# Summing four value pages of sample attention in four column strips of the matrix array

## The chip, the cores and the metric

One Trainium2 chip, one of its cores. The metric is the device time of one execution in microseconds (us), lower is better. Before the change three executions took 3119.28, 3115.47 and 3117.53 us: median 3117.53.

## The reference, cut to what matters

One step of a hybrid decoder layer: 2048 prompt tokens and 8 sample tokens go through the same weights (input projection, an RG-LRU group and a differential-attention group, output projection, gated FFN, gated per-layer embeddings). The change lies in the attention of the 8 sample tokens against their paged cache. Each has 4 pages of 128 past tokens, 4 heads, and 128 values per head:

```python
v_past = cache_v[i][page_table].reshape(db, n_pages * PAGE_SIZE, ATT_HEADS, 2 * ATT_HD)
...
w = probs(q1, k1) - lam * probs(q2, k2)
return jnp.einsum('bhqk,bkhe->bqhe', w, v.astype(jnp.float32))
...
o = _rmsnorm(o, lw['subln_g'], eps=1e-5) * (1.0 - lam_init)
```

So for each sample token (a "row" below) and each head, the output is a weighted sum of 512 cached value vectors and of the token's own, then normed over its 128 elements.

## The kernel before, in words

The kernel has three stages: `project` (input projection, LRU), `attend_first` (attention of the first 512 prompt tokens) and `feed` (output projection, FFN and embeddings of all four groups of 512 tokens, with the attention of groups 1 to 3 and of the samples woven in). The change is in `feed`, which runs from about 679 us to the end.

`feed` writes the order of the work out by hand. `ALL` is a list of 345 items: for each group i the items `mix0`, `mix1`, `mix1t`, `near`, `far`, `gate`/`up` of each FFN block b, `down` of each part, `proj`, `pg`. Each engine's program loops over n, the index in `ALL`, and issues its share of item n. On TensorE an ordinary item is 24 products into the four banks `c_bank` (L2613), each item needing one new weight chunk of 128x1024 elements, of which TensorE takes high and low halves: ScalarE rounds a chunk to its high half (L2041), VectorE subtracts to get the low half (L2292), SyncE loads it two items ahead (L1860).

Into this list two other pieces of work are hung by item number:

- Sample attention. `MULT_S` places the score products, `SOFT` = 18 the softmax, and `VAL_S` = 21, 22, 24, 25, 27, 28, 30, 31 the value products of sample rows 0 to 7, each ahead of that item's own products. `FINISH` = 31. For each row there are four f32 matmuls, one for each page: stationary `wz[:, b, j]` (128 keys x 32, only row b's four columns non-zero), moving `pages` (128 keys x 512 = 4 heads x 128 values), all accumulated in `OT[0:32]`, one half of the PSUM tensor `b_S` (L2885). The profile shows two MATMUL instructions for each of these f32 matmuls, 64 in all. Partition r of the result is row r // 4, head r % 4; all four heads' values stand in it and only a quarter is wanted.
- At item `FINISH` VectorE multiplies `OT[0:32]` by a 0/1 tile `head` and sums over the four head positions (L2577, L2579), adds the token's own value (L2581), squares and sums (L2583, L2584). At `FINISH + 1` ScalarE takes the root (L2258), VectorE inverts and scales (L2587, L2588). At `FINISH + 2` TensorE transposes (L2889) and VectorE scales into `res` (L2591). At `FINISH + 3` SyncE stores `res` (L1990).
- SyncE loads the value pages into three buffers: those of row b + 3 are issued at item `VAL_S[b]` + 1 once row b's matmuls are done (L1895).
- Prompt attention of groups 1 to 3. Its 144 steps (group g, head h, tile t, key block kc) are hung as "ticks" on `PLACES`, the `gate`, `up`, `down` and first `pg` items of groups 0 to 2:

```python
PLACES = [n for n in PLACES if n > FINISH + 3]
tick_at = {PLACES[k * len(PLACES) // NTICK]: k for k in range(NTICK)}
```

With 171 places and 150 ticks, 21 places stay without a tick. Tick k computes the scores of step k at the head of its item (L2905, L2907), the maximum (L2499) and the exponential (L2219); half way through the item the weights of an earlier step (2, 3 or 4 ticks before for g = 1, 2, 3) are transposed (L2917, which waits for VectorE's L2492), split by ScalarE and VectorE (L2233, L2517) and at the end of the item multiplied with the values (L2931, L2933, which wait for L2517). One and two ticks after a tile's last value product its output is gathered; at every fourth tile (a "head end") ScalarE takes a root (L2246, with a table load), VectorE scales all four tiles (L2539) and TensorE transposes them at the start of the next tick (L2866). There are 12 head ends. In `gate` items VectorE and ScalarE also carry the SwiGLU of the `up` item before (L2404, L2406, L2238, L2521, L2119).

At the head of `feed` VectorE clears some tiles and makes `pair` and `head` out of the identity (L2279 to L2286).

Of the kernel before, what the change touches and what calls it, by code (L numbers as in the profile page):

```python
# [10 lines left out]
ALU = mybir.AluOpType  # L11
ACT = mybir.ActivationFunctionType
AX = mybir.AxisListType.X

P = 128
# [5 lines left out]
NS = 8  # L21
# [5 lines left out]
HEADS = 4  # L27
# [5 lines left out]
PAGES = 4  # L33
# [1354 lines left out]
def feed(nc, io, split, sems, pool_turn, shared, early, cached, first_stored):  # L1388
# [4 lines left out]
    ident, ident_r, mask, nlam, sub_gain = shared  # L1393
    w, raw, mixA, raw_in, split_hi, split_ready = early
    pages, qb, table, table_in, pages_in, qb_in, free = cached
# [89 lines left out]
    PLACES = [n for n, (i, item) in enumerate(ALL) if i < LAST and (item[0] in ("gate", "up", "down") or item[:2] == ("pg", 0))]  # L1485
    R, RH, W = NS * COMP, NS * HEADS, HEADS * P
# [1 line left out]
    SOFT = MULT_S[-1] + 1  # L1488
    VAL_S = [SOFT + 3 + 3 * b // 2 for b in range(NS)]
    FINISH = VAL_S[-1]  # L1490
    PLACES = [n for n in PLACES if n > FINISH + 3]
    tick_at = {PLACES[k * len(PLACES) // NTICK]: k for k in range(NTICK)}
    assert len(tick_at) == NTICK
    step_of_value = {s + LAG(s): s for s in range(NSTEP)}
# [74 lines left out]
    with ctx:  # L1569
        top = [nc.sbuf_base + -nc.sbuf_base % 64]  # L1570

        def sb(name, shape, dt=F32, offset=None):
            size = int(np.prod(shape[1:])) * (2 if dt == mybir.dt.bfloat16 else 4)
            if offset is None:
                offset, top[0] = top[0], top[0] + size + -size % 32
            return nc.alloc_sbuf_tensor_at(name, shape, dt, offset=offset)
# [27 lines left out]
        p = sb("b_p", [P, PRING, 2, 512])  # L1604
        wT = sb("b_wT", [P, 2, 512], F32R)
        o = sb("b_o", [P, TILES, P])
# [22 lines left out]
        v32 = sb("d_v32", [RH, P])  # L1629
# [3 lines left out]
        cp = sb("d_cp", [P, PAGES * R])  # L1633
        wz = sb("d_wz", [P, NS, PAGES, RH])
        pair = sb("d_pair", [R, RH])
        head = sb("d_head", [RH, HEADS])
        wo = sb("d_wo", [RH, 1])
        mine = sb("d_mine", [RH, HEADS, P])
        os_ = sb("d_o", [RH, P])
        osq = sb("d_osq", [RH, P])  # L1640
        d_ss = sb("d_ss", [RH, 1])
# [202 lines left out]
        def _(sp):  # L1844
# [74 lines left out]
            for n, (i, item) in enumerate(ALL):  # L1919
                if item == ("mix0", 1):  # L1920
                    wait_if_any(sp, x2_ready, TILES * i)
                    for t in range(2):
                        load_row(x_v, i, t)
                    if i == LAST:

                        sp.wait_ge(stored, 16 * NH)
                        sp.dma_start(s_xr[:], x_s).then_inc(s_in, 16)
                        sp.dma_start(s_pin[:], p_s).then_inc(s_in, 16)
                if item == ("mix1", 0) and i:
                    sp.wait_ge(y_ready, TILES * i)  # L1930
                    load_gain(1)
                if item == ("mix1t", 3):
                    sp.wait_ge(x1_ready, nth(i, 0))
                    load_row(x_v, i, 2)
                if item == ("near", 0):
                    sp.wait_ge(x1_ready, nth(i, 1))
                    load_row(x_v, i, 3)
                if item == ("gate", 2):
                    sp.wait_ge(hn_ready, TILES * i + len(tiles(i)))
                    for k in (2, 3):  # L1940
                        load_gain(k)
                if item == ("gate", 10):
                    for t in range(2):
                        load_p(i, t)
                    sp.wait_ge(x1_out, 16 * (TILES * i + TILES))
                    for t in range(2):
                        load_row(x1_v, i, t)
                if item in (("gate", 18), ("gate", 19)):
                    t = item[1] - 16
                    bank, count = job[i, "pT", t - 2]  # L1950
                    sp.wait_ge(acc_done[bank], count)
                    load_p(i, t)
                if item in (("downt", 3), ("proj", 0)):
                    t = 2 if item[0] == "downt" else 3
                    sp.wait_ge(x2_ready, nth(i, t - 2))
                    load_row(x1_v, i, t)
                if item == ("pg", 0, 3) and i < LAST:
                    sp.wait_ge(x2_ready, TILES * i + TILES)
                    load_gain(0)
                if n:  # L1960
                    for x in range(4, NT):
                        if item_of_score[last_step[x - 4]] == n - 1:
                            load_q(x)
                    for x in range(4, len(kv)):
                        if item_of_score[last_use[x - 4]] == n - 1:
                            load_k(x)
                        if item_of_value[last_use[x - 4]] == n - 1:
                            load_v(x)
                if n + 2 < len(ALL):
                    for e in SPLITS[n + 2]:  # L1970
                        load_entry(e)
                for b in range(NS):
                    if n == MULT_S[b] + 1:
                        if b + 2 < NS:
                            load_qb(b + 2)
                        load_pages(b + 3)
                    if n == VAL_S[b] + 1 and b + 3 < NS:
                        load_pages(NS + b + 3)
                if n == 20:
                    for x in range(4):  # L1980
                        load_k(x)
                if n == FINISH + 1:
                    sp.wait_ge(vs_done, NS)
                    for x in range(4):
                        load_q(x)
                        load_v(x)
                if n == FINISH + 3:
                    sp.wait_ge(res_ready, 1)
                    for h in range(HEADS):
                        sp.dma_start(io["mixT"][LRU + h * P:LRU + h * P + P, SEQ:SEQ + NS], res[:, h]).then_inc(res_out, 16)  # L1990
                if (i, item) == (1, ("gate", 1)):
                    sp.wait_ge(res_out, 16 * HEADS)
                    sp.dma_start(s_mix[:], mix_v[:, :, SEQ:]).then_inc(s_in, 16)
# [37 lines left out]
        def _(act):  # L2031
# [69 lines left out]
            for n, (i, item) in enumerate(ALL):  # L2101
# [151 lines left out]
                if n == SOFT + 2:  # L2253
                    act.wait_ge(from_pe, 2)
                    A.activation(cp[:], PT[:, 0:PAGES * R], ACT.Copy).then_inc(from_act, 1)
                if n == FINISH + 1:
                    act.wait_ge(to_act, 2)
                    A.activation(ors[:], d_ss[:], ACT.Sqrt, bias=eps[0:RH, 2:3], scale=1.0 / P).then_inc(from_act, 1)  # L2258
                if last and kind == "down" and item[2] == 0 and item[3] < 2:
# [16 lines left out]
        def _(dve):  # L2276
            V = nc.vector
# [5 lines left out]
            V.memset(eps[:, 2:3], EPS_SUBLN).then_inc(eps_set, 1)  # L2283
            V.memset(wz[:], 0.0)
            V.reduce_sum(pair[:], ident[0:R, 0:R].rearrange("p (r c) -> p r c", c=2), axis=AX)
            link(V.reduce_sum(head[:], ident[0:RH, 0:RH].rearrange("p (b h) -> p h b", h=HEADS), axis=AX))  # L2286

            def split_second(e):
                n = entry[e]
# [91 lines left out]
            for n, (i, item) in enumerate(ALL):  # L2381
# [192 lines left out]
                    link(V.tensor_copy(wo[:], PT[0:RH, 2 * P:2 * P + 1]))  # L2574
                if n == FINISH:
                    dve.wait_ge(vs_done, NS)
                    link(V.tensor_tensor(mine[:], OT[0:RH].rearrange("p (h e) -> p h e", h=HEADS),  # L2577
                                         head[:].rearrange("p (h o) -> p h o", o=1).broadcast_to([RH, HEADS, P]), ALU.mult))
                    link(V.reduce_sum(os_[:], mine[:].rearrange("p h e -> p e h"), axis=AX))  # L2579

                    link(V.scalar_tensor_tensor(os_[:], v32[:], wo[:], os_[:], ALU.mult, ALU.add))  # L2581

                    link(V.tensor_tensor(osq[:], os_[:], os_[:], ALU.mult))  # L2583
                    V.reduce_sum(d_ss[:], osq[:], axis=AX).then_inc(to_act, 1)  # L2584
                if n == FINISH + 1:
                    dve.wait_ge(from_act, 3)
                    link(V.reciprocal(ors[:], ors[:]))  # L2587
                    V.tensor_scalar(os_[:], os_[:], ors[:], None, ALU.mult).then_inc(to_pe, 1)  # L2588
                if n == FINISH + 2:
                    dve.wait_ge(from_pe, 3)  # L2590
                    V.tensor_scalar(res[:].rearrange("p h b -> p b h"), PT[:, 0:RH].rearrange("p (b h) -> p b h", h=HEADS), sub_gain[:], None, ALU.mult).then_inc(res_ready, 1)  # L2591
                if last and kind == "down" and item[2] == 0 and item[3] < 2:
                    b0, b1 = PARTS[item[1]]
# [12 lines left out]
        def _(pe):  # L2606
# [253 lines left out]
            for n, (i, item) in enumerate(ALL):  # L2860
# [18 lines left out]
                for b in range(NS):  # L2879
                    if n == VAL_S[b]:  # L2880
                        if b == 0:
                            pe.wait_ge(to_pe, 2)
                        pe.wait_ge(pages_in[(NS + b) % 3], 16 * PAGES * ((NS + b) // 3 + 1))
                        for j in range(PAGES):
                            ins = T.matmul(OT[0:RH], wz[:, b, j], pages[:, (NS + b) % 3, j], start=b == 0 and j == 0, stop=b == NS - 1 and j == PAGES - 1)  # L2885
                        ins.then_inc(vs_done, 1)
                if n == FINISH + 2:
                    pe.wait_ge(to_pe, 3)
                    T.transpose(PT[:, 0:RH], os_[:], ident[0:RH, 0:RH]).then_inc(from_pe, 1)  # L2889
                s = scored(n)  # L2890
                if s is not None:
# [138 lines left out]
```

## Time and profile before

| | before |
|---|---|
| median of three executions | 3117.53 us (3115.47 to 3119.28) |
| profiled execution: span from first to last instruction | 3117.8 us |
| TensorE MATMUL busy | 2956.7 us, 95% of the span |
| VectorE busy | 1790.1 us, 57% |
| ScalarE busy | 1359.8 us, 44% |
| GpSimd busy | 231.0 us, 7% |
| mean granted TensorE clock | 0.975 of full |
| DMA | 402.59 MB, mean 129 GB/s |

For the profiled execution the page gives its span alone, and no time around it. A line of a timeline gives start, duration, engine, line of the kernel, operation, output<-inputs, shapes (for TensorE first the rows*columns of the array in use) and how many instructions are merged; in brackets the idle time ahead and who ended it. A busy interval of a MATMUL includes its way through the array, so back-to-back matmuls overlap and their starts are the better clock.

### The profile page before, as it was taken

How to read it: one execution, taken by the hardware profiler on the slowest of the kernel's cores; microseconds unless marked ns; L12 is line 12 of the kernel's file. 1: busy time of each engine (PE TensorE's matmuls, PEld its weight loads, DVE VectorE, ACT ScalarE, POOL GpSimd, SP SyncE). 2: the span in 40 equal slices, each digit the busy share in tenths (PEclk: the TensorE clock that was granted, in tenths of full speed). 3: DMA queues.
4: the chain of work that ended last, by engine and by line, in shares of the span. 5: the costliest groups of instructions: out<-in, count | busy, mean ns of one | idle time of the engine just before them, and what ended most of it. 6: DMA issues, size and time to landing. Idle time of an engine off the chain costs nothing.

```text
span 3117.8 us, 38463 instructions
## 1 busy us (share of the span) xinstructions
PE 2956.7 (95%) x14384; PEld 2402.1 (77%) x14384; DVE 1790.1 (57%) x2858; ACT 1359.8 (44%) x2499; POOL 231.0 (7%) x314
## 2 busy tenths in 40 slices
PE   7999999768999999999999999999999999999997
PEld 6778787557678777777888778788788777787875
DVE  6767746357426666566566665655666555334454
ACT  5654625344224444454444444544444443222233
POOL 0201100110000110001011000011110000000000
PEclk9999989879999999999999999999999999999998
DMA  5536432837654443544443435535342244232221
GB/s 178 187 131 231 134 129 78 237 120 221 194 151 112 115 115 115 176 134 122 124 115 107 117 95 171 157 101 149 88 119 81 92 159 132 84 95 86 80 77 53
DMA packets 377576, 402.59 MB, mean 129 GB/s; under 512 B 25641, under 2 KB 277845, under 8 KB 377392
## 3 DMA queue, kind: packets, MB, share of 16 engines
q1 hardware_dynamic: 360624, 341.32, 37.1%
q0 software_dynamic: 16768, 58.81, 5.3%
q8 instruction: 116, 1.90, 0.2%
q14 instruction: 68, 0.56, 0.1%
HBM read 341.19 MB, written 58.91 MB: 128 GB/s over the span
## 4 chain that ended last, share of the span: by engine, by line
PE 56%; DVE 13%; ACT 5%; issue 3%; POOL 1%; DMA 0%; SPq 0%; ACTq 0%; DVEq 0%; POOLq 0%
PE c_bank L2613 45%; PE b_S L2905 3%; PE b_O L2931 2%; DVE c_w L2292 2%; DVE b_m L2499 2%; PE b_S L2622 1%; ACT b_p L2219 1%; PE b_WT L2917 1%; PE b_O L2622 1%; DVE c_rows L2303 1%; ACT c_junk L2062 1%; DVE b_p L2492 1%; DVE c_rows L2310 1%; PE b_S L2885 1%; DVE b_wT L2517 1%
## 5 line engine op out<-in xcount | busy, mean ns | idle before, releaser
L2613 PE MATMUL c_bank<-c_hT,c_w 128*128 128x512 f32 (+1 forms) x4416 | 1026.8, 386 | 15.3 <-DVE c_hT L2330 15.3
L2613 PEld LDWEIGHTS c_bank<-c_hT,c_w 128*128 128x128 f32 x4416 | 796.9, 190 | 171.0 <-issue 18.2
L2613 PE MATMUL c_bank<-c_w,c_fT 128*128 128x512 f32 x2112 | 508.6, 393 | 0.0
L2292 DVE TENSOR_TENSOR c_w<-c_raw,c_w 128x1024 fp32r<-128x1024 f32 x334 | 405.0, 1220 | 166.1 <-ACT c_w L2041 164.8
L2041 ACT ACTIVATE c_w<-c_raw 128x1024 fp32r<-128x1024 f32 x334 | 351.8, 1057 | 258.3 <-PE c_bank L2613 225.9
L2613 PEld LDWEIGHTS c_bank<-c_w,c_fT 128*128 128x128 f32 x2112 | 390.5, 188 | 86.5 <-issue 3.4
L2219 ACT ACTIVATE b_p<-b_S,b_nm 128x512 f32<-128x512 f32 (+3 forms) x288 | 180.3, 631 | 592.6 <-DVE b_nm L2500 592.6
L898 PE MATMUL a_bank<-a_w,a_hT 128*128 128x512 f32 (+1 forms) x1224 | 300.2, 401 | 0.0
L2613 PE MATMUL c_bank<-c_w,c_hT 128*128 128x512 f32 x1152 | 276.2, 396 | 7.8 <-DVE c_w L2292 4.0
L898 PEld LDWEIGHTS a_bank<-a_w,a_hT 128*128 128x128 f32 (+1 forms) x1224 | 220.7, 183 | 61.2 <-issue 3.8
L2613 PEld LDWEIGHTS c_bank<-c_w,c_hT 128*128 128x128 f32 x1152 | 218.5, 191 | 55.7 <-DVE c_w L2292 5.3
L898 PE MATMUL a_bank<-a_hT,a_w 128*128 128x512 f32 (+2 forms) x1152 | 219.3, 348 | 4.4 <-DVE a_hT L727 4.2
L2006 POOL TENSOR_SCALAR b_p<-b_p,b_coef 128x512 f32<-128x512 f32 (+3 forms) x144 | 128.1, 905 | 1265.6 <-DVE b_coef L2534 1265.1
L898 PEld LDWEIGHTS a_bank<-a_hT,a_w 128*128 128x128 f32 x1152 | 185.6, 199 | 35.8 <-issue 8.3
L2517 DVE TENSOR_TENSOR b_wT<-b_WT,b_wT 128x512 fp32r<-128x512 f32 (+3 forms) x144 | 90.0, 625 | 210.4 <-ACT b_wT L2233 210.4
L2404 DVE SCALAR_TENSOR_TENSOR c_act<-c_act,c_bank 128x512 f32<-128x512 f32 x88 | 60.4, 687 | 232.4 <-PE c_bank L2613 216.1
L2499 DVE TENSOR_REDUCE b_m<-b_S 128x2 f32<-128x1024 f32 (+3 forms) x144 | 156.3, 1085 | 45.3 <-PE b_S L2905 23.5
L2905 PE MATMUL b_S<-b_k,b_q 128*128 128x512 f32 (+3 forms) x576 | 155.8, 386 | 0.0
L2931 PE MATMUL b_O<-b_v,b_wT 128*128 128x256 f32 x504 | 127.7, 326 | 15.3 <-DVE b_wT L2517 14.9
L2931 PEld LDWEIGHTS b_O<-b_v,b_wT 128*128 128x128 f32 x504 | 94.5, 188 | 36.3 <-DVE b_wT L2517 31.8
L2492 DVE SCALAR_TENSOR_TENSOR b_p<-b_p,b_coef 128x512 f32<-128x512 f32 (+3 forms) x144 | 108.0, 750 | 13.1 <-POOL b_p L2006 13.1
L2933 PE MATMUL b_O<-b_v,b_wT 128*128 128x128 f32 x504 | 112.2, 223 | 0.0
(363 smaller groups left out, 3306.2 us busy)
## 6 DMA issues: line engine op xcount, KB each, us to landing
c_raw<-in_ffn_w_gate SPq DMA_DIRECT2D x88, 512.0 KB, 4.9
c_raw<-in_ffn_w_up SPq DMA_DIRECT2D x88, 512.0 KB, 4.2
c_raw<-in_ffn_w_down SPq DMA_DIRECT2D x88, 512.0 KB, 4.2
a_raw<-in_w_in SPq DMA_DIRECT2D x40, 1024.0 KB, 5.2
b_k<-split_kT SPq DMA_DIRECT2D x72, 256.0 KB, 4.9
b_v<-split_v SPq DMA_DIRECT2D x36, 512.0 KB, 3.6
c_raw<-in_w_out SPq DMA_DIRECT2D x32, 512.0 KB, 5.2
c_raw<-in_ple_w_gate SPq DMA_DIRECT2D x32, 512.0 KB, 4.3
```

What stands on the lines that cost most here:

```text
L898: ins = nc.tensor.matmul(out, lhs(k, a), rhs(k, b), start=first and k == 0 and n == 0, stop=end and k == blocks - 1 and n == 2)
L2006: nc.gpsimd.tensor_scalar(part, part, coef[:, x % TRING, 1, kc:kc + 1], 1.0, ALU.mult, ALU.mult).then_inc(t2_ready, 1)
L2041: A.activation(w[:, e[1] % SLOTS, 0], raw[:, n % RAW], ACT.Copy).then_inc(split_hi, 1)
L2219: A.activation(p[:, s % PRING, c, 0:size(s)], S[:, c, 0:size(s)], ACT.Exp, bias=nm[:, x % TRING, c, kc:kc + 1], scale=QSCALE, accum_out=ls ...
L2292: V.tensor_tensor(w[:, e[1] % SLOTS, 1], raw[:, n % RAW], w[:, e[1] % SLOTS, 0].bitcast(F32), ALU.subtract).then_inc(split_ready, 1)
L2492: V.scalar_tensor_tensor(p[:, s % PRING, 0, 0:c], p[:, s % PRING, 0, 0:c], coef[:, x % TRING, 0, kc:kc + 1], p[:, s % PRING, 1, 0:c], ALU. ...
L2499: link(V.reduce_max(m[:, x % TRING, :, kc], S[:, :, 0:size(s)], axis=AX))
L2517: V.tensor_tensor(wT[:, 1, 0:size(s)], WT[:, 0:size(s)], wT[:, 0, 0:size(s)].bitcast(F32), ALU.subtract).then_inc(wt_lo, 1)
L2613: ins = T.matmul(out, lhs(k, a), rhs(k, b), start=first and k == 0 and n == 0, stop=end and k == blocks - 1 and n == 2)
L2905: ins = T.matmul(S[:, z, 0:cols], qq[:, x % 4, a, z], kk[:, c % 4, z, 0:cols], start=a == 0, stop=a == 1 and kc < g)
L2931: T.matmul(O[:, 0].rearrange("p a e -> p (a e)"), wT[:, 0, c * P:c * P + P], vv[:, y % 4, c].rearrange("p a e -> p (a e)"), start=kc == 0 ...
L2933: ins = T.matmul(O[:, 0, 0], wT[:, 1, c * P:c * P + P], vv[:, y % 4, c, 0], start=False, stop=kc == g and c == size(s) // P - 1)
```

## The change

Matmul j of each row writes partitions 32j to 32j + 31 of `OT` instead of all four accumulating in partitions 0 to 31: the four partial sums of the pages stand in four column strips of the array and four partition blocks of the bank. VectorE picks the heads over all 128 partitions and hands `parts` (128x128) to TensorE; a new matmul with `fold` (128x32, ones where p % 32 = r) sums the four blocks into `PT[0:32, 0:128]`; VectorE goes on from there. What followed is one item later each, and the first place for a tick is `FINISH + 5` instead of `FINISH + 4`, so that 170 places are left for 150 ticks; 79 of the 144 score ticks come to lie on another item.

```diff
-    PLACES = [n for n in PLACES if n > FINISH + 3]
+    PLACES = [n for n in PLACES if n > FINISH + 4]
...
-        head = sb("d_head", [RH, HEADS])
+        head = sb("d_head", [P, HEADS])
+        fold = sb("d_fold", [P, RH])
+        parts = sb("d_parts", [P, P])
...
-        mine = sb("d_mine", [RH, HEADS, P])
+        mine = sb("d_mine", [P, HEADS, P])
...
-                if n == FINISH + 3:
+                if n == FINISH + 4:
                     sp.wait_ge(res_ready, 1)
...
-                if n == FINISH + 1:
+                if n == FINISH + 2:
                     act.wait_ge(to_act, 2)
                     A.activation(ors[:], d_ss[:], ACT.Sqrt, bias=eps[0:RH, 2:3], scale=1.0 / P).then_inc(from_act, 1)
...
-            link(V.reduce_sum(head[:], ident[0:RH, 0:RH].rearrange("p (b h) -> p h b", h=HEADS), axis=AX))
+            V.reduce_sum(head[:], ident[:].rearrange("p (b h) -> p h b", h=HEADS), axis=AX)
+            link(V.reduce_sum(fold[:], ident[:].rearrange("p (j r) -> p r j", r=RH), axis=AX))
...
                 if n == FINISH:
                     dve.wait_ge(vs_done, NS)
-                    link(V.tensor_tensor(mine[:], OT[0:RH].rearrange("p (h e) -> p h e", h=HEADS),
-                                         head[:].rearrange("p (h o) -> p h o", o=1).broadcast_to([RH, HEADS, P]), ALU.mult))
-                    link(V.reduce_sum(os_[:], mine[:].rearrange("p h e -> p e h"), axis=AX))
-
-                    link(V.scalar_tensor_tensor(os_[:], v32[:], wo[:], os_[:], ALU.mult, ALU.add))
+                    link(V.tensor_tensor(mine[:], OT.rearrange("p (h e) -> p h e", h=HEADS),
+                                         head[:].rearrange("p (h o) -> p h o", o=1).broadcast_to([P, HEADS, P]), ALU.mult))
+                    V.reduce_sum(parts[:], mine[:].rearrange("p h e -> p e h"), axis=AX).then_inc(to_pe, 1)
+                if n == FINISH + 1:
+                    dve.wait_ge(from_pe, 3)
+                    link(V.scalar_tensor_tensor(os_[:], v32[:], wo[:], PT[0:RH, 0:P], ALU.mult, ALU.add))
...
-                if n == FINISH + 1:
+                if n == FINISH + 2:
                     dve.wait_ge(from_act, 3)
...
-                if n == FINISH + 2:
-                    dve.wait_ge(from_pe, 3)
+                if n == FINISH + 3:
+                    dve.wait_ge(from_pe, 4)
...
-                            ins = T.matmul(OT[0:RH], wz[:, b, j], pages[:, (NS + b) % 3, j], start=b == 0 and j == 0, stop=b == NS - 1 and j == PAGES - 1)
+                            ins = T.matmul(OT[j * RH:j * RH + RH], wz[:, b, j], pages[:, (NS + b) % 3, j], start=b == 0, stop=b == NS - 1)
                         ins.then_inc(vs_done, 1)
-                if n == FINISH + 2:
+                if n == FINISH + 1:
                     pe.wait_ge(to_pe, 3)
+                    T.matmul(PT[0:RH, 0:P], fold[:], parts[:], start=True, stop=True).then_inc(from_pe, 1)
+                if n == FINISH + 3:
+                    pe.wait_ge(to_pe, 4)
                     T.transpose(PT[:, 0:RH], os_[:], ident[0:RH, 0:RH]).then_inc(from_pe, 1)
```

## Rows read from the trace of the kernel before

**Rows 1.** The page: the engines' busy time, and the chain that ended last.

```profile
PE 2956.7 (95%) x14384; PEld 2402.1 (77%) x14384; DVE 1790.1 (57%) x2858; ACT 1359.8 (44%) x2499; POOL 231.0 (7%) x314
PE 56%; DVE 13%; ACT 5%; issue 3%; POOL 1%; DMA 0%; SPq 0%; ACTq 0%; DVEq 0%; POOLq 0%
```

**Rows 2.** Busy time by stretch: length, PE, PEld, DVE, ACT, POOL, clock, DMA, GB/s.

```profile
800.00:921.00 121.00, 121.00 (x468) 80.42 (x468) 31.40 (x50) 29.41 (x39) 0.00 (x0) 1.00 0.60 165
```

**Rows 3.** Timeline of PE around the value products, 809 to 911 us.

```profile
809.10 5.73 PE L2613 MATMUL c_bank<-c_hT,c_w 128*128 128x512 f32 x24
814.76 3.62 PE L2885 MATMUL b_S<-d_pages,d_wz 128*32 128x512 f32 x8
818.31 5.73 PE L2613 MATMUL c_bank<-c_hT,c_w 128*128 128x512 f32 x24
...
895.57 3.62 PE L2885 MATMUL b_S<-d_pages,d_wz 128*32 128x512 f32 x8
899.12 11.17 PE L2613 MATMUL c_bank<-c_w,c_fT 128*128 128x512 f32 x48
910.23 0.24 PE L2889 MATMUL b_S<-ident,d_o 32*128 32x32 f32 x1
```

**Rows 4.** Durations (ns, min/median/max) on L2885, and two weight loads within row 0.

```profile
L2885 PE MATMUL b_S<-d_pages,d_wz x64: 592/592/617, 814.8 to 898.6; 128*32 128x512 f32 x64
...
815.21 0.11 PEld L2885 LDWEIGHTS b_S<-d_pages,d_wz 128*32 128x32 f32 x1 [0.32 <-issue]
815.64 0.11 PEld L2885 LDWEIGHTS b_S<-d_pages,d_wz 128*32 128x32 f32 x1 [0.32 <-issue]
```

**Rows 5.** Timeline of VectorE behind the last value row.

```profile
899.23 0.68 DVE L2577 TENSOR_TENSOR d_mine<-b_S,d_head 32x512 f32<-32x512 f32 x1 [10.39 <-PE b_S L2885]
899.94 1.06 DVE L2579 TENSOR_REDUCE d_o<-d_mine 32x128 f32<-32x512 f32 x1
...
903.23 0.27 DVE L2588 TENSOR_SCALAR d_o<-d_o,d_ors 32x128 f32<-32x128 f32 x1
```

**Rows 6.** Timeline of ScalarE in the same stretch.

```profile
902.03 0.29 ACT L2258 ACTIVATE d_ors<-d_ss,c_eps 32x1 f32<-32x1 f32 x1 [3.94 <-DVE d_ss L2584]
...
910.83 2.00 ACT L2041 ACTIVATE c_w<-c_raw 128x1024 fp32r<-128x1024 f32 x2
912.85 1.28 ACT L2119 ACT_TABLE_LOAD   x1
916.14 0.60 ACT L2119 ACTIVATE c_act<-c_bank 128x512 f32<-128x512 f32 x1 [2.02 <-PE c_bank L2613]
```

**Rows 7.** SyncE's queue: the last value pages, the store of res, the loads behind.

```profile
866.84 4.03 SPq L1895 DMA_DIRECT2D d_pages<-in_cache_v  x4
...
913.58 2.63 SPq L1990 DMA_DIRECT2D scratch_mixT<-d_res  x4
916.25 0.43 SPq L1860 DMA_DIRECT2D c_raw<-in_ffn_w_gate  x1
```

**Rows 8.** VectorE at the head of the last stage.

```profile
680.49 0.18 DVE L2286 TENSOR_REDUCE d_head<-ident 32x4 f32<-32x32 f32 x1
688.56 1.23 DVE L2295 TENSOR_TENSOR c_hT<-c_raw,c_hT 128x1024 fp32r<-128x1024 f32 x1 [7.89 <-ACT c_hT L2046]
```

**Rows 9.** Windows from score to score: an ordinary tick, then five of head ends.

```profile
1490.68:1498.46 7.78, 7.78 (x42) 6.56 (x42) 2.48 (x4) 4.18 (x10) 0.00 (x0) 1.00 0.24 67
1001.25:1010.03 8.78, 8.36 (x47) 7.00 (x46) 4.56 (x8) 3.97 (x10) 1.46 (x2) 1.00 0.53 179
1010.03:1019.00 8.97, 6.79 (x37) 5.45 (x35) 4.56 (x10) 5.85 (x12) 0.60 (x1) 1.00 0.37 117
1080.18:1086.81 6.63, 6.63 (x36) 5.47 (x35) 3.37 (x12) 5.15 (x10) 0.59 (x1) 1.00 0.52 158
1452.02:1461.85 9.83, 8.35 (x46) 6.93 (x46) 6.25 (x11) 4.49 (x11) 0.38 (x1) 1.00 0.46 160
1461.85:1470.86 9.01, 8.32 (x43) 6.44 (x42) 4.99 (x7) 6.29 (x10) 1.82 (x2) 1.00 0.25 89
```

## The prediction

> **What bounds the kernel now.** I read the page first. TensorE is busy 95% of the span and holds the largest part of the chain that ended last [rows 1]. Then I read busy time by stretch, for the 121 us in which all eight rows of value products lie: TensorE is busy in every one of the 121.00 us, at the full granted clock, VectorE for 31 and ScalarE for 29 [rows 2]. So here a microsecond less on TensorE is a microsecond less of the kernel, until something else is late. The timeline of TensorE gives the price of a row: its eight instructions start at 814.76 and the next c_bank group at 818.31, 3.55 us, and the last row is the same, 895.57 to 899.12 [rows 3]. Eight rows are 28.4 us, 0.9% of the span, and that is all the change can touch. The c_bank products between rows are the same before and after.
>
> Inside a row the weight loads start 0.43 us apart (815.21, 815.64) [rows 4], so a pass of 512 columns takes 0.43 us of the array, and 8 x 0.43 = 3.44 leaves 0.11 for getting in and out of the 32-column form. Two passes belong to each f32 matmul, and both passes of a matmul use one strip. The shape field says 128*32 already before the change [rows 3]: the change makes no pass smaller, so a gain can only come from passes that run side by side.
>
> **The change, part by part.**
>
> *The value products.* No row of this trace has two matmuls in different column strips, so the gain has to be bounded. Nearest end one: nothing overlaps, 8 passes one behind another as now, gain 0. Nearest end two: only the two passes of one matmul stay apart and all four strips run together, 2 x 0.43 + 0.11 = 0.97 us a row instead of 3.55, gain 2.58 x 8 = 20.6 us. Between them: the passes are issued in program order, strip 0 first, strip 0 second, strip 1 first, and so on. The second pass of strip 0 can start only after the first (0.43 us); the first pass of strip 1 may start along with it; the second pass of strip 1 needs the strip again and waits for 0.86. So only 3 of 8 passes hide: 5 x 0.43 + 0.11 = 2.26 us, and something for three starts that follow another. A weight load takes 0.11 us [rows 4]; at nothing per start a row saves 1.29, at 0.11 each it saves 0.96. The starts of the loads, 0.43 apart and each 0.11 long, show that a load is done behind a running pass, so I take the upper part: 1.2 a row, **9.6 us** for eight. I take the middle and not either end because starts in this trace never pass each other, yet nothing in a strip's own work should hold another strip.
>
> The Trainium skill ("TensorE: Matmul & The Clock Gate", Part 3) gives 3.07 times for four row tiles and 2.38 times for three column tiles, and says that matmuls are strictly first in, first out. Its factor of four tiles would make 28.4 us into an estimated 9.3, a gain of 19.1; its order rule, with two passes a matmul, gives the middle case. No run here shows either. Against the change speaks "TensorEngine Tiling (Array Packing)", Key Properties: changing the tiling mode drains the array, changing the tile does not. By it nothing is added here, since the form was 128*32 before.
>
> *The matmul with fold*, two passes of 128 columns: 2 x 0.43 / 4 = 0.21, plus the 0.11 of going in and out: **+0.3 us** on TensorE's path, at item 32. What it waits for, the head pick and the sum over heads, ends at 899.94 + 1.06 = 901.0 [rows 5], on 128 partitions as on 32, since the length per partition is the same. Item 32 starts 5.55 us after 899.12, at 904.7: 3.7 us of cover. If that were gone the wait would be paid one for one.
>
> *VectorE* waits at item 32 for fold. Queued behind it are only the weight halves of item 33, which wait for ScalarE until 911 anyway. The root moves from 902.03 to item 33 and now stands behind ScalarE's two weight halves that end at 912.83, plus a table load of 1.28 and the root of 0.29 [rows 6]: 914.4. VectorE's reciprocal and scaling (0.27 for the latter [rows 5]) make it about 914.9. TensorE wants it for the transpose at item 34, which starts one item after 910.23 [rows 3], at 915.9. A cover of 1.0 us, thin but there; ScalarE's next tanh is at 916.14 [rows 6], and one more table load ends before it. I cost both at 0; were the cover gone, a few tenths.
>
> *SyncE* has the four stores of res one item later. They take it 2.63 us, and the load behind them went out at 916.25 [rows 7]; after, that load goes first, the stores fall in the idle time behind it. The first tick, where ScalarE waits for their landing, moves by one item too. 0. *Value pages*: the last four are issued by 870.9 [rows 7] and used at 895.57 [rows 3]; DMA is at 0.60 in the stretch [rows 2]. Nine us less leave 15 us. 0.
>
> *The head of the stage*: VectorE gets one more reduction of about the 0.18 us of its neighbour, and then idles 7.89 us [rows 8]. 0.
>
> *The ticks.* This is the part that the title does not tell of. Dropping place 35 moves 79 of 144 ticks, nearly all by one item, mostly from gate to up or back. An ordinary tick costs 7.78 us with no stall [rows 9], wherever it lies. Stalls come at head ends. Of two ticks with the same products, the second tick of a head end took 8.97 on a gate item with 2.2 us of TensorE idle (length less busy), and 6.63 on a down item with none [rows 9]: 2.3 us for the kind of item, since VectorE and ScalarE carry the SwiGLU beside it. A first tick on gate is 9.83, 2.0 over the 7.78, one on up 8.78, 1.0 over; a second tick on up is 9.01, 1.2 over, of which four transposes of a quarter pass each are 0.4 [rows 9]. Six of twelve head ends change their kinds (first tick, second tick): two of group 1 go from (up, gate) to (gate, up), about -0.3 each since 1.0 + 2.3 becomes 2.0 + 0.8 and a little; one from (down, down) to (down, gate), +2.4; one from (gate, up) to (up, down), -1.2; one from (gate, up) to (gate, gate), +1.4; one (up, gate) of group 3 to (gate, up), -0.6. The sum is +1.4. Ticks behind these give some back. I take **+1 us**, with -3 and +5 as the ends, since the second-tick stalls for one kind differ by a microsecond between groups.
>
> **The sum**: -9.6 + 0.3 + 1 = -8.3 us against the span of 3117.8: 3109.5. The median of the runs is 0.3 below that span, less than the runs differ, so I leave it at 3109.5. A measurement of this kernel can tell 0.2%, 6.2 us, from no change; the forecast is just past it.
>
> **The rivals.**
>
> 1. *All four strips run together, the pair order does not matter.* Then -20.6 + 0.3 + 1 = -19.3: 3098. For it: nothing but the bound; the page's factor would give an estimated 3100. Against: starts in program order, and two passes in one strip.
>
> 2. *Strips do not overlap at all for f32 data*, because the array takes one moving stream at a time. Then +0.3 + 1: 3119, no change to be seen; with the ends of the ticks 3116 to 3123. For it: f32 passes take 0.43 us for 512 columns, twice the 0.23 of the c_bank products (24 in 5.55 us), so the moving side is already the slow one; and no row shows an overlap. This is also the case in which the change does not do what it says.
>
> 3. *Slower: a strip change drains.* At each of the 24 changes of strip inside rows the next pass waits until the one before has left the array (its 592 ns less the 0.43 between starts, 0.16) and its weights are not loaded behind it (0.11 [rows 4]): 24 x 0.27 = 6.5, + 0.3 + 1: 3125.6. It decides from (6.2 - 1.3) / 24 = 0.20 us per change. For it: getting in and out of the 32-column form costs 0.11 now. Against: that is for two changes of form, and 0.11 for both is well below 0.20 for one.
>
> **How the numbers follow.** The middle case gets 0.50, all strips 0.12, no overlap 0.28, drain 0.10. The middle case spans 7.7 to 10.3 of gain and -3 to +5 of ticks, 3105 to 3115: two thirds of it is faster by over 0.2%, the rest is not. Faster: 0.50 x 0.67 + 0.12 = 0.46. Slower: most of the drain case and a little of no overlap, 0.11. Same: 0.43. The range leaves out the far end of rival 1 and of rival 3: 3098 to 3122.
>
> **What would show it.** Starts on L2885: pairs with one start together with the pass before, a row 2.3 us from its first start to the next c_bank start (rival 1: under 1.2; rival 2: 3.55; rival 3: over 4). One pair of passes from fold at item 32 without idle ahead, the transpose at item 34 without idle. TensorE's lengths from score to score behind the first tick must sum to about 1 us more than before; if that sum is off by more than 5, the ticks decided and not the strips. I would be wrong on the whole if TensorE showed idle between 800 and 921 us.

## The result, and the profile after

The changed kernel takes 3089.55 us (median of 4 executions, 3085.45 to 3091.51); the kernel before, with a fourth execution beside them, 3116.5 us (3110.3 to 3119.28). The ratio is 0.991, 95% interval 0.9896 to 0.9925: 27.0 us less by the medians. I had forecast 3109.5 within 3098 to 3122.

| | before | after |
|---|---|---|
| profiled execution: span | 3117.8 us | 3086.5 us |
| time of the profiled execution | not given | 3088.24 us |
| TensorE MATMUL busy | 2956.7 us | 2932.9 us |
| mean granted TensorE clock | 0.975 | 0.975 |
| first start of a value row to first score of tick 0 | 814.76 to 921.39: 106.6 us | 809.96 to 902.27: 92.3 us |
| score of tick 0 to score of tick 143 | 1492.9 us | 1481.5 us |

The timeline of TensorE after, columns as in [rows 3]; line numbers from here on are those of the kernel shown, 4 higher than before around the value products (L2889 is the L2885 of before, L2893 the matmul with fold, L2896 the transpose):

```profile
809.96 1.06 PE L2889 MATMUL b_S<-d_pages,d_wz 128*32 128x512 f32 x8
810.96 5.74 PE L2617 MATMUL c_bank<-c_hT,c_w 128*128 128x512 f32 x24
...
872.95 1.07 PE L2889 MATMUL b_S<-d_pages,d_wz 128*32 128x512 f32 x8
873.94 5.74 PE L2617 MATMUL c_bank<-c_w,c_fT 128*128 128x512 f32 x24
879.61 0.41 PE L2893 MATMUL b_S<-d_parts,d_fold 128*32 128x128 f32 x2
879.95 5.73 PE L2617 MATMUL c_bank<-c_w,c_fT 128*128 128x512 f32 x24
885.52 5.60 PE L2617 MATMUL c_bank<-c_hT,c_w 128*128 128x512 f32 x24
891.05 0.24 PE L2896 MATMUL b_S<-ident,d_o 32*128 32x32 f32 x1
```

A row now takes 809.96 to 810.96, **1.00 us** instead of the 3.55 of [rows 3]: 2.55 less, 20.4 for eight. No line has idle ahead of it. Two more views, the duration of one instruction and the weight loads of row 0, help to tell how (a PEld line is TensorE loading weights):

```profile
L2889 PE MATMUL b_S<-d_pages,d_wz x64: 592/604/617, 810.0 to 873.4; 128*32 128x512 f32 x64
...
809.96 0.16 PEld L2889 LDWEIGHTS b_S<-d_pages,d_wz 128*32 128x32 f32 x8 [0.35 <-issue]
```

A pass (one of the two MATMUL instructions that the profile shows for each f32 matmul) lasts as long as before: 592 to 617 ns against 592 to 617. The profile models the ends of matmuls, so this alone is weak; the starts below say the same. All eight weight loads of the row are done within 0.16 us, where before they came 0.43 us apart from the third on [rows 4]. The pass groups show the rest: in short windows of the same timeline the row splits into two fours,

```profile
809.96 0.64 PE L2889 MATMUL b_S<-d_pages,d_wz 128*32 128x512 f32 x4
...
810.41 0.61 PE L2889 MATMUL b_S<-d_pages,d_wz 128*32 128x512 f32 x4
```

four passes that run together, one per strip, and 0.45 us later the four others. With 0.43 us for the second four and 0.12 us until the next group starts, that is the whole 1.00.

The chain that ended last has more TensorE in it (59% against 56%) and less VectorE (11% against 13%) than in [rows 1]. The run with the ticks alone (below) has the same 59% and 11%, so this shift comes from the ticks and not from the strips:

```profile
PE 59%; DVE 11%; ACT 5%; issue 2%; POOL 0%; DMA 0%; SPq 0%; ACTq 0%; DVEq 0%; POOLq 0%
```

Where did the 31.3 us between the two profiled spans go? (a) The last stage starts earlier: its first product at 674.91 instead of 679.03, and the first value row 4.8 us earlier. No matmul up to there is touched by the change; in the eight profiles of this study the first product lies anywhere from 673.4 to 679.0 us and the first value row from 807.1 to 814.8, and the profile before has the latest of both. I take this part for spread, not effect. (b) From the first value row to tick 0: 106.6 - 92.3 = 14.3, and tick 0 lies one item of 5.54 us later, so 19.9 us come from the rows and fold. (c) From tick 0 to tick 143: 11.3, less the 5.54 of the item that the first tick moved past, so 5.8 us, where I had forecast 1 us more. (d) The rest, behind the last tick, 0.8.

### The profile page after: what moved, and what is told of

It is laid out like the page before. It is cut to its first block, busy times and chain, and to the rows that moved or that the text cites. A ratio compares the mean times of both kernels' runs of the same rounds, so it can differ in the third digit from the quotient of the medians.

```text
span 3086.5 us, 38468 instructions
## 1 busy us (share of the span) xinstructions
PE 2932.9 (95%) x14386; PEld 2394.3 (78%) x14386; DVE 1793.5 (58%) x2859; ACT 1358.1 (44%) x2499; POOL 232.7 (8%) x314
## 4 chain that ended last, share of the span: by engine, by line
PE 59%; DVE 11%; ACT 5%; issue 2%; POOL 0%; DMA 0%; SPq 0%; ACTq 0%; DVEq 0%; POOLq 0%
PE c_bank L2617 47%; PE b_S L2912 3%; PE b_O L2938 2%; DVE c_w L2295 2%; PE b_S L2626 1%; PE b_WT L2924 1%; PE b_O L2626 1%; DVE b_m L2502 1%; ACT c_junk L2064 1%; DVE c_rows L2306 1%; ACT b_p L2221 1%; DVE c_rows L2313 1%; DVE b_p L2495 1%; PE b_O L2940 1%; DVE c_hT L2333 1%
## 5 line engine op out<-in xcount | busy, mean ns | idle before, releaser
L2617 PEld LDWEIGHTS c_bank<-c_hT,c_w 128*128 128x128 f32 x4416 | 798.3, 191 | 171.2 <-issue 19.1
L2938 PE MATMUL b_O<-b_v,b_wT 128*128 128x256 f32 x504 | 127.2, 325 | 11.5 <-DVE b_wT L2520 11.3
```

Source lines behind the costliest of these rows:

```text
L2617: ins = T.matmul(out, lhs(k, a), rhs(k, b), start=first and k == 0 and n == 0, stop=end and k == blocks - 1 and n == 2)
L2938: T.matmul(O[:, 0].rearrange("p a e -> p (a e)"), wT[:, 0, c * P:c * P + P], vv[:, y % 4, c].rearrange("p a e -> p (a e)"), start=kc == 0 ...
```

## The experiments

**One part of the change alone.** Two kernels take the change apart. The first is the kernel before with the new places for the ticks only:

```diff
-    PLACES = [n for n in PLACES if n > FINISH + 3]
+    PLACES = [n for n in PLACES if n > FINISH + 4]
```

> The kernel before with one edit: the first place for a tick is FINISH + 5 instead of FINISH + 4, so that the ticks lie as in the changed kernel; the value products stay in one strip. Theory (the ticks themselves gain): TensorE's lengths from score to score sum to some 6 us less than before, as they do in the changed kernel, and the time falls by 5 to 8 us, to about 0.998 of before. Rival (the ticks cost about +1 us as I forecast, and what the changed kernel gained there is the spread of runs): time within 2 us of before, and the second ticks of the head ends as long as before. A row of value products takes 3.55 us under both.

Measured: 3106.62 us against 3115.76, ratio 0.9975 (0.9965 to 0.9984): 7.8 us less by the ratio, 9.1 by the medians. The times by score, tick 0 to 143, sum to 5.6 us less than before (5.54 for the moved item taken off), and tick for tick they agree with the changed kernel within 0.1 us, but for ticks 35, 48 and 89, which differ by 0.7 to 1.6 us. The rival falls: the ticks themselves gain.

The second is the changed kernel with that line turned back:

```diff
-    PLACES = [n for n in PLACES if n > FINISH + 4]
+    PLACES = [n for n in PLACES if n > FINISH + 3]
```

> The changed kernel with one edit undone: the first place for a tick is FINISH + 4 again, so the ticks lie as before; strips and fold stay. Theory: a row takes 1.00 us, eight rows and fold save 20.0 us, the ticks take the same as before, so 20 us less than before (0.9936). Rival (the strips also change something behind them, a wait or the clock, which makes up the 6.6 us): 26 us less (0.9917). Tick 0 may wait a few tenths for the store of res, which is now only one item ahead.

Measured: 3097.23 us against 3115.76, ratio 0.9935 (0.9921 to 0.9949): 20.3 us less by the ratio, 18.5 by the medians. The rival's 0.9917 lies outside the interval. Its first value row starts at 809.21 and tick 0 at 896.09, on the same item as before: 86.88 us against 106.63, 19.75 less. Row and fold:

```profile
809.21 1.07 PE L2889 MATMUL b_S<-d_pages,d_wz 128*32 128x512 f32 x8
810.21 5.74 PE L2617 MATMUL c_bank<-c_hT,c_w 128*128 128x512 f32 x24
...
878.86 0.41 PE L2893 MATMUL b_S<-d_parts,d_fold 128*32 128x128 f32 x2
879.20 5.74 PE L2617 MATMUL c_bank<-c_w,c_fT 128*128 128x512 f32 x24
```

The two parts add up: 0.9975 x 0.9935 = 0.9910, the ratio of the whole change. No third cause is needed; one of a few us could still hide in the intervals.

The ticks of this run lie where they did before, and yet they sum to 1.7 us more. Tick 11 waits 2.2 us for the same tile in both traces and takes 8.97 us before, at a granted clock of 1.00, and 10.54 us here, at 0.84. So the length of a single tick can differ by 1.6 us between two traces of the same order of work.

**How the strips overlap.** The profile shows starts, but not which pass stands in which strip. Two strips of two pages each tell it apart, once blocked and once in turns (the cut shows the blocked one):

```diff
-  ins = T.matmul(OT[j * RH:j * RH + RH], wz[:, b, j], pages[:, (NS + b) % 3, j], start=b == 0, stop=b == NS - 1)
+  ins = T.matmul(OT[j // 2 * RH:j // 2 * RH + RH], wz[:, b, j], pages[:, (NS + b) % 3, j], start=b == 0 and j % 2 == 0, stop=b == NS - 1 and j % 2 == 1)
...
-  T.matmul(PT[0:RH, 0:P], fold[:], parts[:], start=True, stop=True)
+  T.matmul(PT[0:RH, 0:P], fold[0:2 * RH], parts[0:2 * RH], start=True, stop=True)
```

(head pick and sum likewise on 64 partitions; in turns it is `j % 2 * RH`, started at j < 2, stopped at j > 1).

> The changed kernel with two strips instead of four: pages 0 and 1 go to strip 0, then pages 2 and 3 to strip 1, in this program order; head pick and fold on 64 partitions. Theory (each strip has a queue of its own, and a strip's passes do not wait for program order across strips): 4 passes x 0.43 + 0.13 = 1.85 us a row. Rival (passes start in program order and only overlap with a neighbour in another strip): strip 1 can start only with the last pass of strip 0, 7 x 0.43 + 0.13 = 3.14 us. Rival (page pairs run in lockstep, any two matmuls): the same 1.85, which the run with turns tells apart.

> As the run before with two strips, but taken in turns: pages 0 and 2 in strip 0, 1 and 3 in strip 1, in program order 0, 1, 2, 3. Theory (own queues): 1.85 us a row again. Rival (program order of all passes, two passes to a matmul): 5 to 6 passes, 2.3 to 2.7 us. Rival (only neighbours in program order overlap, whole matmuls): 1.85 here but 3 passes of matmuls, 2.7, in the blocked order.

Measured, blocked:

```profile
808.57 1.92 PE L2889 MATMUL b_S<-d_pages,d_wz 128*32 128x512 f32 x8
810.42 5.78 PE L2617 MATMUL c_bank<-c_hT,c_w 128*128 128x512 f32 x24
...
808.57 0.15 PEld L2889 LDWEIGHTS b_S<-d_pages,d_wz 128*32 128x32 f32 x4 [0.35 <-issue]
809.03 0.12 PEld L2889 LDWEIGHTS b_S<-d_pages,d_wz 128*32 128x32 f32 x2 [0.31 <-issue]
```

and in turns:

```profile
810.20 1.91 PE L2889 MATMUL b_S<-d_pages,d_wz 128*32 128x512 f32 x8
812.04 5.78 PE L2617 MATMUL c_bank<-c_hT,c_w 128*128 128x512 f32 x24
```

1.85 and 1.84 us. In the blocked order strip 1's first pass comes fifth in the program, behind four passes of strip 0, and still the row is four passes long; four weights are loaded at once at the start, then two at a time. So each strip takes its own passes as soon as it is free, and a row costs the number of passes in its fullest strip: 8 passes 3.55, 4 passes 1.85, 2 passes 1.00, close to 0.43 x passes + 0.14. The rivals fall: program order gives 3.14 blocked and 2.3 to 2.7 in turns, neighbours alone give 2.7 blocked, and page pairs 0 with 2 and 1 with 3 in lockstep, possible in the blocked order, share a strip in turns. (Program order is that in which the kernel issues the matmuls. The lines of the profile carry no place in the program, so what lets a strip's passes go by those of the other, or where on the way to the array that happens, is not shown.) The times of these two, one execution each, are 3094.03 and 3095.06, as 0.85 us more for each of eight rows would have it within the spread.

**What a tick costs where.** A "first tick" of a head end is the one in which ScalarE takes the root, the "second" the one at whose start TensorE transposes the head. In the prediction I had sorted items by name. Looking again at the same ticks in six traces, another sorting fits: whether the item *follows an up item* (or `far`), because that item carries VectorE's and ScalarE's SwiGLU. Gate 8 and gate 16 follow a `down` and carry none; the first `down` of a part follows an up and carries it. For the second tick of a head end the length over its own TensorE work (estimated from like ticks) then sorts so: behind an up 2.0 to 4.0 us, elsewhere -0.4 to 1.3; for the first tick 2.0 to 2.9 (0.3 at gate 10 where the item behind it is free and takes up the stall) against 0.3 to 1.3. Tick 35, which reaches over the border of two groups, is left out. To test it, one free place moved:

```diff
-    tick_at = {PLACES[k * len(PLACES) // NTICK]: k for k in range(NTICK)}
+    FREE = (47, 52, 61, 69, 99, 107, 116, 124, 133, 141, 150, 164, 188, 196, 205, 213, 222, 230, 239, 253)
+    tick_at = {n: k for k, n in enumerate(n for n in PLACES if n not in FREE)}
```

(the changed kernel's own free places, with 47 in place of 44.)

> The changed kernel with one free place moved: item 47 (gate 15) stays without a tick instead of item 44 (gate 14). Only ticks 8, 9 and 10 move, each one item earlier; the first tick of the first head end goes from gate 15, an item behind an up, to up 14, and the second stays on up 15. Theory (a head end costs by whether the item carries the SwiGLU of an up before it, whatever its own name): the lengths of ticks 8, 9 and 10 less 5.54 for each item go from 3.09, about 2.2 and 4.30 to about 2.2, 2.2 and 3.2, so about 2 us less for these ticks and nothing elsewhere. Rival (the stalls only move on to the next ticks, since ScalarE and VectorE have the same work to do): ticks 11 and 12 get longer by what 8 to 10 lose, and the sum over ticks 8 to 15 stays within 0.5 us.

Measured, lengths less 5.54 per item: tick 8 from 3.10 to 2.54, tick 9 from 2.01 to 2.00, tick 10 from 4.29 to 2.58; ticks 11 to 15 within 0.06 us of before. The sum over 8 to 15 is 2.3 us less. The stall does not move on. Tick 10 was cheaper by more than I said, tick 8 dearer. Elsewhere three ticks that had not moved (31, 60 and 89) differ by 0.7 to 1.6 us, both ways; the last section comes back to 60 and 89. The one execution took 3083.76 us.

This run does not test the kind of item alone. Tick 10 also got a free item behind it, and that by itself can take a stall away: tick 59 of the changed kernel lies on gate 10, behind an up, with a free item behind it, and takes 2.59, as little as tick 10 here on up 14 (2.58). Without a free item behind it tick 10 takes 4.29 on gate 15 (changed kernel) and 3.24 on up 14 (before). So of the 1.7 us that tick 10 lost, about 1.05 can be the kind of item and the rest the free item, or the free item did it all.

Then all free places were chosen so:

```diff
+    FREE = (47, 49, 65, 78, 97, 103, 107, 129, 133, 147, 151, 164, 167, 183, 193, 205, 211, 215, 224, 233)
+    tick_at = {n: k for k, n in enumerate(n for n in PLACES if n not in FREE)}
```

> The changed kernel with its 20 free places chosen by hand instead of by even spacing, so that nearly all first and second ticks of head ends lie on items that follow no up item (gate 15 and 20 of group 0, gate 4, 6, 13, 15, 18, 20 of group 1, gate 6, 8, 11, 13, 18 of group 2 and seven more stay free). Theory (the ticks' stalls are set by the kind of item, and add up): adding the lengths of like ticks in the six traces so far gives 22 us less than the changed kernel; as some like ticks were seen once or not at all I expect 10 to 22 less, 0.984 to 0.988 of before. Rival (stalls only move on): within 3 us of the changed kernel, 0.990 to 0.992 of before.

Measured: **3068.98 us** (3064.48 to 3071.36) against 3114.42, ratio 0.9852 (0.9834 to 0.987). That beats the changed kernel (0.991, interval 0.9896 to 0.9925) by 0.6%, some 18 us, with the same work in another order; both ratios are against the kernel before, the two were not run side by side. The waits of TensorE behind 860 us, in total, times, and the longest, before:

```profile
PE b_O L2931 <- DVE b_wT L2517: 14.9, 30, 0.8
PE b_WT L2917 <- DVE b_p L2492: 12.6, 11, 2.5
...
PE b_WT L2866 <- DVE b_o L2539: 7.2, 8, 1.5
```

in the changed kernel:

```profile
PE b_O L2938 <- DVE b_wT L2520: 11.3, 23, 0.8
PE b_WT L2924 <- DVE b_p L2495: 9.8, 10, 2.3
PE b_WT L2870 <- DVE b_o L2542: 8.6, 7, 1.8
```

and with the free places by hand:

```profile
PE b_O L2939 <- DVE b_wT L2521: 8.4, 18, 0.6
...
PE b_WT L2871 <- DVE b_o L2543: 4.1, 4, 1.5
...
PE b_WT L2925 <- DVE b_p L2496: 3.3, 5, 0.9
```

The three waits of a tick shrink from 34.7 to 29.7 to 15.8 us. All of TensorE's idle time between tick 0 and tick 143 is 48.3, 42.5 and 30.5 us. One tick shows the mechanism, the second of a head end in group 2 (tick 60). In the changed kernel it lies on gate 11, behind up 10; ScalarE, VectorE and TensorE in their order:

```profile
1538.20 0.69 ACT L2111 ACTIVATE b_oT<-b_WT,sub_gain 128x512 f32<-128x512 f32 x1 [4.58 <-PE b_WT L2870]
1538.91 1.28 ACT L2121 ACT_TABLE_LOAD   x1
1540.20 0.60 ACT L2121 ACTIVATE c_act<-c_bank 128x512 f32<-128x512 f32 x1
...
1540.91 0.69 DVE L2407 SCALAR_TENSOR_TENSOR c_act<-c_act,c_bank 128x512 f32<-128x512 f32 x1 [6.03 <-ACT c_act L2121]
1541.63 0.69 DVE L2409 SCALAR_TENSOR_TENSOR c_act<-c_act,c_bank 128x512 f32<-128x512 f32 x1
1542.23 1.22 DVE L2295 TENSOR_TENSOR c_w<-c_raw,c_w 128x1024 fp32r<-128x1024 f32 x1
1543.37 0.75 DVE L2495 SCALAR_TENSOR_TENSOR b_p<-b_p,b_coef 128x512 f32<-128x512 f32 x1
...
1544.17 0.66 PE L2924 MATMUL b_WT<-ident,b_p 128*128 128x128 f32 x4 [2.33 <-DVE b_p L2495]
```

and by hand it lies on up 10, right behind tick 59 on gate 10 (gate 11 behind it carries tick 61):

```profile
1527.98 1.23 DVE L2296 TENSOR_TENSOR c_w<-c_raw,c_w 128x1024 fp32r<-128x1024 f32 x1 [2.42 <-ACT c_w L2044]
1529.12 0.86 DVE L2496 SCALAR_TENSOR_TENSOR b_p<-b_p,b_coef 128x512 f32<-128x512 f32 x1
...
1530.03 0.66 PE L2925 MATMUL b_WT<-ident,b_p 128*128 128x128 f32 x4
```

Read the first from the end: TensorE waits 2.33 us for `b_p`; VectorE could not start it before 1543.37, because its order puts the two SwiGLU operations and a weight half ahead; these wait for ScalarE's tanh, which waits for the gathering of the head and for a table load of 1.28 us (the profile shows one more table load at 1531.08, ahead of the head's root). `b_p` starts 5.45 us behind the first score of the tick. By hand it starts 3.09 us behind it: only the weight half stands ahead of it, and TensorE does not wait for `b_p`.

For the second ticks this is the kind of item: ticks 48 and 60, moved off the items behind an up, become 2.3 and 3.0 us shorter (0.7 of the 3.0 goes with the clock, see below) and cost what they did before the change. For the first ticks (10, 26, 83, 100 and 116, 1.7 to 2.0 us shorter each) the kind and the free item behind them changed together, and no run parts the two. Nor is "follows no up" enough: tick 132 went from a `down` to gate 16, which follows a `down`, and became 1.28 us longer. There VectorE first adds the `down` result into `c_rows`,

```profile
2275.47 2.47 DVE L2356 TENSOR_TENSOR c_rows<-c_rows,c_bank 128x512 f32<-128x512 f32 x4
```

and starts the tick's maximum 2.94 us behind its first score instead of 1.66.

## Why the prediction was wrong, point by point

- *What bounds the stretch* was right: TensorE is busy in all 107.00 us from 795 to 902 after the change as well, and what its matmuls save is saved.

```profile
795.00:902.00 107.00, 107.00 (x495) 80.15 (x494) 35.98 (x55) 30.90 (x41) 0.00 (x0) 1.00 0.67 190
```

- *The value products, 9.6 us*: **the step that failed first.** I took the passes as started in program order, so that the second pass of strip 0 would hold strip 1 and only 3 of 8 passes would hide. Measured 20.4: six of eight hide, rival 1, which I gave 0.12, at 0.97 us a row against 1.00. The reason I gave against it, that starts in the trace never pass each other, rested on a trace in which all value products used the same strip, and so could show nothing about it; the runs with two strips showed that strips do not wait for each other. The Trainium skill's factor for four row tiles in "TensorE: Matmul & The Clock Gate", Part 3 (3.07, an estimated 19.1 us) was far nearer than my sum; here the factor is 3.55 / 1.00 = 3.55, for four column strips. Its rule that matmuls are strictly first in, first out is not borne out by the blocked run for passes in different strips.
- *Fold, 0.3 us*: 879.61 to 879.95, 0.34. Right. Its input was ready at 874.80 + 1.08 = 875.9, 3.7 us before its start, as said.
- *The chain behind fold, 0*: right. The scaling ended at 889.09 + 0.28 = 889.4 and the transpose started without idle at 891.05, a cover of 1.7 us where I had 1.0: a weight half that I had put ahead of the root stands behind it.

```profile
887.28 1.28 ACT L2260 ACT_TABLE_LOAD   x1
888.58 0.29 ACT L2260 ACTIVATE d_ors<-d_ss,c_eps 32x1 f32<-32x1 f32 x1
888.78 1.04 ACT L2043 ACTIVATE c_w<-c_raw 128x1024 fp32r<-128x1024 f32 x1
```

- *SyncE, value pages, the head of the stage, 0 each*: no wait of TensorE answers to any of them; SyncE stored `res` at 891.64 behind the load at 891.11, as said.
- *The ticks, +1 us*: **the step that failed second**, in sign. Alone they gave 7.8 us less by the runs and 5.6 by the trace. I priced head ends by the item's name, and charged 2.4 us to the one that went from `down` to gate 16. Gate 16 follows a `down`; that tick stayed as long as before. For the first part of group 1 I charged 0.8 us to a second tick on an up item; it has no stall there at all (ticks 11 and 27 became 2.4 and 2.7 us shorter, against 1.1 and 1.4 more for ticks 10 and 26, which I had foreseen as 1.0). A second tick behind up 7, on a `down`, cost 2.3 to 3.0 more than before, where I had put a stall of 0 on any `down`. (The -1.2 for that head end does not follow from my own prices either: 1.0 less for the first tick and 0.8 less for the second make -1.8.) Tick for tick the head ends (first and second ticks) came to -1.6 us, where I had +1.4, and all other ticks to -4.2, where I had -0.4: their small stalls, which I let cancel, did not (ticks 2, 4, 6, 20, 32 and 33 lost 5.1 us between them).
- *The slower side* (a strip change drains) was excluded outright: a row with three changes of strip takes less than a third of the time of one with none.
- *The range*: it was meant to leave out the far ends of rivals 1 and 3. In fact the middle of rival 3 (3125.6) lay outside and that of rival 1 (3098.5) on its edge, so half of a case that I held possible had no room. The lower end of rival 2 should have been 3115 and not 3116.

Either failure alone would have left the time in the range: 3109.5 - 10.8 = 3098.7 with the strips right, 3102.7 with the ticks right. Together they make 3091.9. The measured 3089.55 is 2.4 us below that and 8.5 below the range; 1.3 of the 2.4 is that I started from the span of one profile, 3117.8, and the median before came out at 3116.5.

## What to carry to other kernels

Four f32 matmuls with 32 columns of weights and 512 moving columns took 1.00 us instead of 3.55 once they wrote four different blocks of 32 partitions: count the passes of the fullest strip, not all passes. When a change shifts work in a hand-written order, price every place by what the other engines do in it (here: does the item carry the activation of the one before, a table load, or additions on VectorE) and by whether the item behind it is free, not by its name; 18 us lay in choosing which items stay free. And a trace that never uses a feature cannot speak against it: the middle of two bounds was the least supported case, not the safest.

## What the hardware showed that I had not expected

The passes of an f32 matmul in one strip do not hold those of another, even when four of them stand ahead of it in the program (1.85 us for four passes in each of two strips, in either order).

The stage ahead of the change ends anywhere between 673.4 and 679.0 us in eight profiles of kernels whose matmuls are alike up to there; a single pair of profiles could have hidden or doubled the effect of the ticks.

After a wait of TensorE the granted clock may fall, and not in every run. Behind the wait of 2.33 us in tick 60 it was 0.84 and then 0.68 of full in the changed kernel; the windows are 1543.00 to 1546.50, the 3.5 us behind, and a narrower one inside, which has the lower of the two levels, 0.50 or 1.2 GHz, throughout (1.00 is 2.4 GHz):

```profile
1543.00:1546.50 3.50, 2.33 (x10) 2.00 (x11) 2.42 (x4) 1.01 (x3) 0.00 (x0) 0.84 0.49 145
1546.50:1550.00 3.50, 3.50 (x16) 2.87 (x16) 2.38 (x3) 2.38 (x5) 0.00 (x0) 0.68 0.02 5
1545.50:1548.50 3.00, 3.00 (x9) 2.32 (x8) 1.05 (x2) 3.00 (x7) 0.00 (x0) 0.50 0.37 111
```

The same tick with the same wait in the run with one free place moved stayed at 1.00 and took 11.26 us instead of 11.98:

```profile
1535.54:1546.80 11.26, 8.32 (x44) 6.45 (x42) 6.03 (x9) 6.92 (x11) 0.98 (x2) 1.00 0.23 72
```

So a stall can cost more than its idle time, by 0.7 us here. Five of the profiles have tick 60 on gate 11: in three its clock was 0.86 and it took 11.96 to 11.98 us, in the two others 1.00 and 11.26. The same may be behind tick 89, 1.6 us longer in the changed kernel than before: the last 13 us of its stretch had a clock of 0.89, the last 12 of it before 1.00. What makes the clock fall in one run and not in the next stays open.
